# Fp32 transformer blocks on one core: the weight sums of the seven-product linears moved from GpSimd to VectorE, and two reorderings on VectorE

## What is computed

```python
D_MODEL = 1024; SEQ = 256; D_FF = 2816
def swiglu(u, w_gate, w_up, w_down):
    return (jax.nn.silu(u @ w_gate) * (u @ w_up)) @ w_down
...
mods = jnp.split(jax.nn.silu(c) @ w_ada[l] + b_ada[l], N_MOD, axis=-1)
sh1, sc1, gt1, sh2, sc2, gt2, sh3, sc3, gt3 = mods
u = modulate(rmsnorm(h, g_ff1[l]), sh1, sc1)
h = h + FFN_RES * gt1[:, None, :] * swiglu(u, w1_gate[l], w1_up[l], w1_down[l])
...  # attention and mLSTM
u = modulate(rmsnorm(h, g_ff2[l]), sh3, sc3)
h = h + FFN_RES * gt3[:, None, :] * swiglu(u, w2_gate[l], w2_up[l], w2_down[l])
```

## Time and profile before

| | us |
|---|---|
| median of 3 runs | 1231.33 |
| the profiled execution | 1231.31 |
| its span, first to last instruction | 1229.5 |
| TensorE (PE) busy | 1195.8 |
| VectorE (DVE) busy | 660.2 |
| ScalarE (ACT) busy | 332.2 |
| GpSimd (POOL) busy | 274.2 |

### The profile page before, as it was taken

The page is one execution under the profiler, slowest core; times in us unless marked ns, Lnnn a source line. Parts: engine busy times, 40 slices in busy tenths (PEclk is TensorE's granted clock), DMA queues, the critical chain, the costliest instruction groups (busy, mean ns, idle before and its releaser), DMA issues.

```text
span 1229.5 us, 20015 instructions
## 1 busy us (share of the span) xinstructions
PE 1195.8 (97%) x8286; PEld 1075.1 (87%) x8286; DVE 660.2 (54%) x1512; ACT 332.2 (27%) x943; POOL 274.2 (22%) x169
## 2 busy tenths in 40 slices
PE   9998989999999999999799997999999999999997
PEld 7888989996688888889799997998888998888887
DVE  4457786372027533351689877557865323157632
ACT  2111210142124434100311210134324421146542
POOL 0008555100012000012356755340000310000101
PEclk9998999999999999999999998999999999999999
DMA  9969838582475555568399965848242563443321
GB/s 346 336 206 315 299 124 266 197 281 78 153 241 149 187 205 188 183 245 280 114 353 313 303 214 194 257 174 283 81 121 73 185 215 117 151 125 104 103 69 35
DMA packets 164139, 241.70 MB, mean 197 GB/s; under 512 B 13921, under 2 KB 112415, under 8 KB 164048
## 3 DMA queue, kind: packets, MB, share of 16 engines
q1 hardware_dynamic: 156160, 230.45, 55.5%
q10 hardware_dynamic: 6784, 5.74, 1.6%
q0 software_dynamic: 1104, 4.22, 1.0%
HBM read 236.82 MB, written 4.62 MB: 196 GB/s over the span
## 4 chain that ended last, share of the span: by engine, by line
PE 90%; DVE 6%; ACT 2%; POOL 1%; DMA 1%; issue 1%; DVEq 0%; ACTq 0%; POOLq 0%
PE ps L189 88%; PE ps L192 2%; DVE arena L198 2%; DVE tmps L204 1%; ACT U L195 1%; ACT tmps L195 1%; POOL arena L198 1%; DVE tmps L198 1%; DVE ABT L198 0%; DMA bias_row<-rows 0%; DMA arena<-bias_row 0%; DVE rstd L216 0%; DVE tmpA L198 0%; ACT arena L195 0%; DVE U L198 0%
## 5 line engine op out<-in xcount | busy, mean ns | idle before, releaser
L189 PE MATMUL ps<-U,slots 128*128 128x256 f32 (+2 forms) x2912 | 538.1, 344 | 0.2 <-DVE arena L198 0.2
L189 PEld LDWEIGHTS ps<-U,slots 128*128 128x128 f32 (+1 forms) x2912 | 465.5, 190 | 52.5 <-issue 5.0
L189 PE MATMUL ps<-arena,slots 128*128 128x128 f32 (+1 forms) x1840 | 272.6, 308 | 11.1 <-DVE arena L198 11.1
L189 PEld LDWEIGHTS ps<-arena,slots 128*128 128x128 f32 x1840 | 252.9, 192 | 27.9 <-DVE arena L198 11.4
L198 POOL TENSOR_TENSOR arena<-slots,arena 128x1024 f32<-128x1024 f32 (+1 forms) x44 | 132.9, 3021 | 125.4 <-DVE arena L198 89.7
L195 ACT ACTIVATE tmps<-ps 128x256 f32<-128x256 f32 (+2 forms) x151 | 57.4, 383 | 373.3 <-PE ps L189 361.4
L207 DVE CUSTOM_DVE_ANT_0 arena<-arena,tmpA 128x1024 f32<-128x1024 f32 x88 | 111.1, 1298 | 16.0 <-DMA arena<-in_w_adaT 15.5
L189 PE MATMUL ps<-arena 128*128 128x128 f32 (+7 forms) x940 | 106.7, 294 | 1.0 <-DVE arena L198 1.0
L189 PEld LDWEIGHTS ps<-arena 128*128 128x128 f32 (+2 forms) x940 | 97.4, 188 | 10.1 <-issue 4.3
L189 PE MATMUL ps<-ABT,arena 128*128 128x128 f32 (+5 forms) x752 | 86.6, 280 | 10.4 <-ACT tmps L195 6.7
L195 ACT ACTIVATE arena<-ps 128x512 f32<-128x512 f32 (+3 forms) x116 | 50.5, 459 | 153.4 <-PE ps L189 149.2
(11 more groups left out here) (181 smaller groups left out, 1097.6 us busy)
## 6 DMA issues: line engine op xcount, KB each, us to landing
slots<-in_w_in SPq DMA_DIRECT2D x14, 2048.0 KB, 9.4
slots<-in_w_down SPq DMA_DIRECT2D x16, 1408.0 KB, 7.9
slots<-in_w_gate SPq DMA_DIRECT2D x18, 1024.0 KB, 8.8
slots<-in_w_up SPq DMA_DIRECT2D x18, 1024.0 KB, 11.7
arena<-in_w_adaT SPq DMA_DIRECT2D x28, 512.0 KB, 5.5
slots<-in_w_adaT SPq DMA_DIRECT2D x7, 2048.0 KB, 8.4
arena<-in_ada_w1T SPq DMA_DIRECT2D x24, 512.0 KB, 9.2
slots<-in_a_in_w SPq DMA_DIRECT2D x6, 2048.0 KB, 10.3
```

The costliest lines, as they stand in the source:

```text
L189: return Nothing() if self.e is None else self.e.matmul(*a, **k)
```

## The change

All of t1 to t4 are made on VectorE (v_t, v_dn_t1, v_dn_t2, v_dn_t34), and the two loops over GpSimd's weight sums leave its program. In v_gu_blocks v_t(b+1) stands right behind the gating of b-1 and all modulation sums of the block behind it. In block 10, t2 of the first down product is made ahead of v_gu, t3 and t4 behind the last activation sums. For down products 1 and 2, t2 to t4 stand behind the modulation sums. In f2's opening v_su comes ahead of the gates. Every wait on GpSimd's results becomes a wait on VectorE's.

```diff
-        def v_t1(e, f, b):
+        def v_t(e, f, b):
@@
             e.tensor_tensor(t[:, 0], w[:, :, 0:4, P:T], w[:, :, 0:4, 0:P], ALU.subtract).then_inc(*dve.up(f, "t1", b))
-
-        def p_t(e, f, b):
-
-            t, w = TG.buf(f, b), gu_block(f, b)
             e.wait_ge(*dve.at(f, "t1", b))
-            e.wait_ge(*arrived(f + " gu", b))
-            e.tensor_tensor(t[:, 1], w[:, :, 4:8, P:T], t[:, 0], ALU.subtract).then_inc(*pool.up(f, "t2", b))
-            e.tensor_tensor(w[:, :, 0:4, P:T], w[:, :, 4:8, P:T], w[:, :, 0:4, P:T], ALU.subtract).then_inc(*pool.up(f, "t3", b))
-            e.wait_ge(*pool.at(f, "t2", b))
-            e.tensor_tensor(t[:, 2], w[:, :, 4:8, 0:P], t[:, 1], ALU.subtract).then_inc(*pool.up(f, "t4", b))
+            e.tensor_tensor(t[:, 1], w[:, :, 4:8, P:T], t[:, 0], ALU.subtract).then_inc(*dve.up(f, "t2", b))
+            e.tensor_tensor(w[:, :, 0:4, P:T], w[:, :, 4:8, P:T], w[:, :, 0:4, P:T], ALU.subtract).then_inc(*dve.up(f, "t3", b))
+            e.wait_ge(*dve.at(f, "t2", b))
+            e.tensor_tensor(t[:, 2], w[:, :, 4:8, 0:P], t[:, 1], ALU.subtract).then_inc(*dve.up(f, "t4", b))
@@
-        def p_dn_t(e, f, p):
+        def v_dn_t2(e, f, p):
@@
             if p:
                 e.wait_ge(*pe.at(f + " dn", "p5", p - 1))
-            e.tensor_tensor(t2, hi[:, :, P:T], t1, ALU.subtract).then_inc(*pool.up(f + " dn", "t2", p))
-            e.tensor_tensor(lo[:, :, P:T], hi[:, :, P:T], lo[:, :, P:T], ALU.subtract).then_inc(*pool.up(f + " dn", "t3", p))
+            e.tensor_tensor(t2, hi[:, :, P:T], t1, ALU.subtract).then_inc(*dve.up(f + " dn", "t2", p))
+
+        def v_dn_t34(e, f, p):
+
+            lo, hi = dn_of(f, p)
+            t2, t4 = (TD[(3 * p + n) % 4] for n in (1, 2))
+            e.tensor_tensor(lo[:, :, P:T], hi[:, :, P:T], lo[:, :, P:T], ALU.subtract).then_inc(*dve.up(f + " dn", "t3", p))
             e.wait_ge(*(pe.at(f + " dn", "p6", p - 1) if p else pe.at(f, "p4", 10)))
-            e.wait_ge(*pool.at(f + " dn", "t2", p))
-            e.tensor_tensor(t4, hi[:, :, 0:P], t2, ALU.subtract).then_inc(*pool.up(f + " dn", "t4", p))
+            e.wait_ge(*dve.at(f + " dn", "t2", p))
+            e.tensor_tensor(t4, hi[:, :, 0:P], t2, ALU.subtract).then_inc(*dve.up(f + " dn", "t4", p))
@@
-                chunks = CHUNKS[f].get(b, [])
-                v_ada_chunks(e, chunks[:2])
                 if b < 10:
-                    v_t1(e, f, b + 1)
+                    v_t(e, f, b + 1)
                 else:
                     v_sd(e, f, 0, 9)
                     v_dn_t1(e, f, 0)
-                v_ada_chunks(e, chunks[2:])
+                    v_dn_t2(e, f, 0)
+                v_ada_chunks(e, CHUNKS[f].get(b, []))
                 v_gu(e, f, b)
             v_gu_act(e, f, 10)
             v_sd(e, f, 9, 11)
+            v_dn_t34(e, f, 0)
@@
                 v_ada_chunks(e, [(8 + p, c) for c in range(4)])
+                if p < 2:
+                    v_dn_t2(e, "f1", p + 1)
+                    v_dn_t34(e, "f1", p + 1)
@@
+            v_su(e, "f2", "n3")
             v_gate(e, "f2", 0, 0)
             v_gate(e, "f2", 1, 0)
             e.wait_ge(*pe.at("sums", "n3", 1))
-            v_t1(e, "f2", 1)
-            v_su(e, "f2", "n3")
+            v_t(e, "f2", 1)
             v_gate(e, "f2", 0, 1)
             v_gate(e, "f2", 1, 1)
@@
         def gpsimd(e):
             p_bias(e)
-            for b in range(5, 11):
-                p_t(e, "f1", b)
-            for p in range(3):
-                p_dn_t(e, "f1", p)
```

More of the change, by code:

```diff
@@ L1097, in t_gu @@
             i.then_inc(*pe.up(f, "p5", b))
-            e.wait_ge(*pool.at(f, "t3", b))
+            e.wait_ge(*dve.at(f, "t3", b))
             e.wait_ge(*act.at(f, "u2", b))
@@ L1106, in t_gu @@
             i.then_inc(*pe.up(f, "p3", b))
-            W.close([pe.now(), pool.at(f, "t4", b)], f + " gu", b)
-            e.wait_ge(*pool.at(f, "t4", b))
+            W.close([pe.now(), dve.at(f, "t4", b)], f + " gu", b)
+            e.wait_ge(*dve.at(f, "t4", b))
             e.wait_ge(*act.at(f, "u3", b))
@@ L1201, in v_dn_t1 @@
             e.tensor_tensor(TD[3 * p % 4], lo[:, :, P:T], lo[:, :, 0:P], ALU.subtract).then_inc(*dve.up(f + " dn", "t1", p))
-        def p_dn_t(e, f, p):
+        def v_dn_t2(e, f, p):
             lo, hi = dn_of(f, p)
-            t1, t2, t4 = (TD[(3 * p + n) % 4] for n in range(3))
+            t1, t2 = TD[3 * p % 4], TD[(3 * p + 1) % 4]
             e.wait_ge(*dve.at(f + " dn", "t1", p))
@@ L1237, in t_dn @@
             e.wait_ge(*dve.at("sd", f))
-            e.wait_ge(*pool.at(n, "t2", p))
+            e.wait_ge(*dve.at(n, "t2", p))
             e.wait_ge(*act.at(n, "s1", p))
@@ L1241, in t_dn @@
             product(C2[:, P:T], t1, SD[:, 0], False).then_inc(*pe.up(n, "p5", p))
-            e.wait_ge(*pool.at(n, "t3", p))
+            e.wait_ge(*dve.at(n, "t3", p))
             e.wait_ge(*act.at(n, "u2", p))
@@ L1247, in t_dn @@
             product(C2[:, P:T], hi[:, :, P:T], SD[:, 3], False).then_inc(*pe.up(n, "p3", p))
-            W.close([pe.now(), pool.at(n, "t4", p)], n, 2 * p + 1)
-            e.wait_ge(*pool.at(n, "t4", p))
+            W.close([pe.now(), dve.at(n, "t4", p)], n, 2 * p + 1)
+            e.wait_ge(*dve.at(n, "t4", p))
             e.wait_ge(*act.at(n, "u3", p))
@@ L3298, in vector @@
             v_gate(e, "f1", 8)
-            v_t1(e, "f1", 5)
+            v_t(e, "f1", 5)
             v_gate(e, "f1", 9)
@@ L3395, in vector @@
                 v_ada_chunks(e, [(25 + p, c) for c in range(4)])
+                if p < 2:
+                    v_dn_t2(e, "f2", p + 1)
+                    v_dn_t34(e, "f2", p + 1)
                 if p == 1:
@@ L3753, in gpsimd @@
             p_bias_rows(e)
[L3754 to L3757, removed]
             p_squares(e, "n4")
```

## The result

The changed kernel takes 1199.45 us (median of 4 runs, 1198.59 to 1201.22); the kernel before, on the same chip, 1231.53 (4 runs). The ratio is 0.9745 with a 95% interval of 0.9728 to 0.9761. The profiled execution took 1198.71, with a span of 1196.9 where before it was 1229.5. First the busy times and the chain by line, as in the earlier trace rows.

A forecast was written before the change was run, and what follows sets the result against it. TensorE was taken as the bound, busy 97% of the span, losing time to idle gaps and a lower clock behind them. Gains of 6.4 + 7.9 + 6.2 + 8.7 = 29.2 us took 1231.3 to 1202.1, range 1198 to 1212.

The forecast's parts named there:

- Part 1: Block 5 of f1: moving t2 to t4 removes the gap ahead of p6 and its clock loss, 6.4 us gained.
- Part 2: Steady blocks: nothing gained or lost, VectorE working 11.1 of 12.5 us with more than 4 us spare before v_gu's limit.
- Part 3: Opening of the down products: 7.9 us gained in f1 and 8.7 in f2, with a 0.7 us gap staying.
- the term for the clock: First down product of each stage: 2.95 us lost to the lower clock behind gaps, counted as regained.
- Part 4: Opening of f2: activation sums first, 4.0 us of gap and 2.2 of clock gained, 6.2 in all.
- The cost of a moved sum: t2 to t4 on VectorE: 1.22 us each taken, up to 3.36 beside GpSimd; 1.62 for sums of 1408 elements.
- Rival A: f2's opening: the clock still falls because 2.85 us stand still in two pieces, 1204.3 us; chance 0.10.
- Rival B: First blocks of f1 or f2: transfers or VectorE come late, two to ten us come back, 1204 to 1212; chance 0.17.
- Rival C: Sixteen blocks: VectorE becomes the bound, slower than before, 1267 us at 3.36 a sum; chance 0.04.
- Rival D: Gaps have a releaser the profile hides, so only the down products gain, 1214.7 us, or nothing does; chance 0.06.

The follow-up runs named there:

- only_b5: The kernel before with only block 5 of f1 changed, its t2 to t4 on VectorE directly behind t1: 1223.3 us, ratio 0.9941.
- dn0_late: The kernel before, with GpSimd starting the first down product's weight sums only behind VectorE's last activation sums, nothing moved: 1222.67 us, ratio 0.9936.
- steady_pool: The changed kernel with t2 to t4 of blocks 6-10 of f1 and 2-10 of f2 on GpSimd again, in the new order: 1212.49 us.
- su_back: The changed kernel with v_su of f2's opening behind v_t(1) again: 1203.75 us, ratio 0.9783.
- extra2: The changed kernel with t4 of 14 steady blocks computed two more times, each with a wait: 1220.65 us, ratio 0.9922.
- extra4: The changed kernel with t4 of 14 steady blocks computed four more times, each with a wait: 1255.42 us, ratio 1.0213.
- only_f2: The kernel before with only f2's opening changed, v_su first and block 1's t2 to t4 on VectorE: 1225.63 us, ratio 0.9953.
- pool_oldorder: The changed kernel with steady blocks' t2 to t4 on GpSimd again and two modulation sums ahead of t1 as before: 1202.77 us, ratio 0.9782.

## Why the prediction was right

The prediction was 1202.1 and the time is 1199.45.

**Part 1** said 6.4 us: 6.48, and only_b5 gets it alone. **Part 2** said nothing gained or lost: the blocks are 12.5 us and unbroken. In block 7 of f1 (T = 112.4) v_gu ends at T+13.9 where I had T+14.2. In block 1 of f2 it ends at T2+4.5 where I had T2+4.7. Weight blocks came in time.

**Part 3** said 7.9 and 8.65: 8.31 and 9.11. The gap that stays is 0.48, not 0.7. The other 0.2 of each is the term for the clock, 2.95 in the sum and 3.14 as it came out in f1 (8.31 less 5.17 of gap), 3.19 in f2. **Part 4** said 4.0 of gap and 2.2 of clock: the gaps shrank by 6.86 - 2.69 = 4.17, and p6 and p5 by 5.98 - 3.81 = 2.17. The two gaps came at 1.37 and 1.32, forecast 1.35 and 1.5.

The working of the sum gives 29.2, the traces 30.6 from p1 of block 5 on: 0.9 is part 3, 0.2 is parts 1 and 4, 0.3 is a gap late in the program that I did not look at. The remaining 2.05 between the two profiles is the start: no term foresaw it, and as far as the runs show it is chance.

**The cost of a moved sum**, the number with the widest bounds (1.22 to 3.36), is 1.22 and 1.62. The reason given, that GpSimd has no work there, held: dn0_late and steady_pool switch the long durations off and on.

**Rival A** didn't come: two gaps of 1.37 and 1.32 left the clock at 1.00. su_back shows a price near the 2.2 that it named, 2.4 us. **Rival B**: no gap stands in a block. **Rival C** did not come, and its arithmetic was off. A round exceeds 12.5 us at 1.22 + 1.0/3 = 1.55 us a sum, not at 1.7, because of the 0.7 us of standing still. The gain is eaten where the loss is 30.6: between extra2 (20.1 us lost in the profile, 2.5 more a block) and extra4 (57.2 lost, 5.0 more), in a straight line at 3.2 a block, or 2.3 us a sum, where I had 2.45. Perfetto Trace Analysis of the Trainium skill ("Optimizing Scalar/DVE Operations") says that with a saturated VectorE it may make sense to offload some work, even to GpSimd, and then warns that between these two it might not help, since they share an SBUF read port. steady_pool offloads to GpSimd, and the trace agrees with the warning: VectorE issues 42 instructions less than in the changed kernel and is busy 680.1 us instead of 652.1. **Rival D** fell with only_b5 and only_f2.

What the prediction had wrong without paying for it is the worth of the steady blocks. It priced moving them at nothing by looking at TensorE's unbroken blocks of before. Leaving them costs 3.3 us in the old order and 13 in the new one, so the part of the edit that looked idle protects the rest.

## What to carry to other kernels

When two engines share a resource, read what each instruction takes alone and beside the other, and cost an edit by the engine's whole round: work moved back to the idle engine can lengthen the busy one. Unbroken blocks on the bounding engine show that a load is hidden in this order of work, not that it is hidden in another, so redo the sum for each reordering. A slack counted for steady blocks is spent at the stage behind them, where the next opening has none.

## What was not expected of the hardware

**A tiny instruction pays like a large one.** In steady_pool an addition of 128x4 elements takes 2.18 us beside GpSimd where it takes 0.16 alone.

```profile
614.84 2.18 DVE L198 TENSOR_TENSOR mods<-mods,vec 128x4 f32<-128x4 f32 x1
```

**The length of a gap alone doesn't tell what the clock does.** Windows of extra4, each right behind a gap ahead of p7:

```profile
630.59:634.30 3.71, 3.71 (x17) 3.71 (x18) 3.64 (x5) 0.13 (x1) 0.00 (x0) 0.50 1.00 344
...
696.47:699.30 2.83, 2.83 (x17) 2.83 (x18) 2.76 (x4) 0.13 (x1) 0.00 (x0) 0.68 0.98 328
712.98:715.00 2.02, 2.02 (x18) 2.02 (x19) 1.99 (x3) 0.12 (x1) 0.00 (x0) 1.00 0.92 287
```

The gaps ahead of them were 3.41, 1.94 and 2.14 us: the granted clock fell to the lower level of 1.2 GHz behind the first, for part of the stretch behind the second, and not at all behind the third, the longer one. Every gap of 3.41 or more in the two swiglus was followed by a lower clock; of the seven between 1.9 and 2.8 in extra2 and extra4, all but the one of 2.14 were. Short gaps are not always harmless either: in the down products, pool_oldorder's pair of 1.24 and 1.00 shown above left 44 matmuls at 5.18 us, while a pair of 1.08 and 1.00 in extra4, with a gap of 2.66 a block earlier, was followed by 6.80:

```profile
170.64 2.69 PE L189 MATMUL ps<-ABT,slots 128*128 128x128 f32 x16 [2.66 <-ACT tmps L195]
183.41 0.71 PE L189 MATMUL ps<-arena,slots 128*128 128x128 f32 x4 [1.08 <-DVE arena L198]
185.13 6.80 PE L189 MATMUL ps<-arena 128*128 128x128 f32 x44 [1.00 <-DVE arena L198]
```

These two pairs suggest that what TensorE did before a gap counts with the gap, and that rival A was nearer than the result looks; one case of each doesn't show it. What exactly decides is open.

**The clock costs nothing where TensorE isn't the bound.** In extra4 the rounds of f2 stay at 16.3 to 16.5 us whether p7 takes 2.02 or 3.75.

**The start of the program has two lengths**, some 2 us apart, as told above (p1 of block 5 at 87.2 to 87.4 or 88.8 to 89.7), with no difference in the code there.
